# Filler products of TensorE and GpSimd's digit memsets moved in the routing stage of a mixture-of-experts layer

## The reference

```python
def moe_ffn(h, w_router, b_router, w1, b1, w2, b2):
    logits = jnp.matmul(h, w_router, preferred_element_type=jnp.float32) + b_router
    top_vals, top_idx = lax.top_k(logits, TOP_K)
    gates = jax.nn.softmax(top_vals, axis=-1)
    e_flat = top_idx.reshape(-1)
    order = jnp.argsort(e_flat, stable=True)
    ...
    def expert_block(args):
        toks, gts, e = args
        xb = h[toks]
        hid = xb @ w1[e] + b1[e]
        yb = clamped_swiglu(hid) @ w2[e] + b2[e]
        return yb * gts[:, None]
```

## Time and profile before

| | us |
|---|---|
| median of 3 runs | 1941.39 |
| lowest, highest | 1940.39, 1941.68 |
| profiled execution | 1941.4 |
| its span, first to last instruction | 1939.6 |
| TensorE busy in the span | 1895.6 |
| VectorE | 1357.6 |
| ScalarE | 415.9 |
| GpSimd | 238.5 |

### The profile page before, as it was taken

One profiled execution on the slowest core, in us unless ns is written; L12 is line 12 of the kernel. 1 busy time (PEld: TensorE's weight loads), 2 busy tenths in 40 slices (PEclk: granted clock), 3 DMA queues, 4 the chain that ended last, 5 costly groups with the idle time before them and its releaser, 6 DMA issues.

```text
span 1939.6 us, 33456 instructions
## 1 busy us (share of the span) xinstructions
PE 1895.6 (98%) x12202; PEld 1384.8 (71%) x12202; DVE 1357.6 (70%) x3838; ACT 415.9 (21%) x925; POOL 238.5 (12%) x319
## 2 busy tenths in 40 slices
PE   8999999997999999999999999999999999999996
PEld 6677777774999999999999999933334444444442
DVE  3777877874467777775666666665548788888785
ACT  2222333323022122222222222222322000001000
POOL 1222122221010011111111111110100000000000
PEclk9999999998999999999999999999999999999998
DMA  9411110014876787778888889889999999999891
GB/s 315 109 43 43 43 43 17 26 33 179 324 223 214 247 269 267 247 260 280 286 293 294 299 300 302 312 298 411 407 400 379 336 324 335 336 338 331 302 326 56
DMA packets 202864, 477.51 MB, mean 246 GB/s; under 512 B 7016, under 2 KB 14228, under 8 KB 196624
## 3 DMA queue, kind: packets, MB, share of 16 engines
q1 hardware_dynamic: 188048, 427.44, 61.2%
q0 software_dynamic: 11312, 39.85, 8.3%
q10 hardware_dynamic: 3452, 9.47, 1.2%
HBM read 449.33 MB, written 27.41 MB: 246 GB/s over the span
## 4 chain that ended last, share of the span: by engine, by line
issue 38%; PE 33%; DMA 4%; POOL 1%; DVE 0%; POOLq 0%; ACT 0%; DVEq 0%
PE ps_unit L1974 32%; DMA out_dram<-y_rows,idx_cur 4%; POOL x_got L1451 1%; PE ps_act L2086 0%; PE ps_list L2086 0%; PE ps_list L1946 0%; POOL carrier L1447 0%; POOL out_dram L1508 0%; POOLq L1144 0%; DVE match L1655 0%; POOLq L1344 0%; PE ps_unit L1954 0%; POOL out_dram L1463 0%; ACT xT L1559 0%; POOLq L1499 0%
## 5 line engine op out<-in xcount | busy, mean ns | idle before, releaser
L1974 PE MATMUL ps_unit<-xT,w_slot 128*128 128x136 f32 (+6 forms) x3840 | 521.5, 298 | 4.1 <-issue 2.6
L1974 PEld LDWEIGHTS ps_unit<-xT,w_slot 128*128 128x128 f32 x3840 | 516.7, 196 | 4.7 <-issue 4.7
L2004 PE MATMUL ps_unit<-w_slot,xT 128*128 128x512 f32 x704 | 306.7, 594 | 0.0
L1333 DVE STREAM_TRANSPOSE xT<-x_got 32x256 f32<-32x256 f32 x644 | 280.3, 435 | 10.6 <-DMA x_got<-h_rows,idx_next 2.2
L1974 PE MATMUL ps_unit<-act_T,w_slot 128*128 128x136 f32 (+6 forms) x1920 | 261.6, 298 | 0.1
L1974 PEld LDWEIGHTS ps_unit<-act_T,w_slot 128*128 128x128 f32 x1920 | 257.9, 190 | 2.2 <-DVE act_T L1736 1.5
L2004 PEld LDWEIGHTS ps_unit<-w_slot,xT 128*128 128x128 f32 x704 | 132.8, 190 | 163.0 <-issue 163.0
L1752 DVE STREAM_TRANSPOSE y_rows<-yT 32x256 f32<-32x256 f32 x372 | 162.0, 435 | 55.1 <-ACT yT L1574 50.2
L976 PE MATMUL ps_c<-hT,w_in_sb 128*128 128x128 f32 x1536 | 181.8, 278 | 3.5 <-DMA w_in_sb<-in_w_in_dram 3.5
L976 PEld LDWEIGHTS ps_c<-hT,w_in_sb 128*128 128x128 f32 x1536 | 176.9, 193 | 8.3 <-issue 4.0
L1447 POOL TENSOR_TENSOR carrier<-carrier 128x1 f32<-128x1 f32 x64 | 14.5, 227 | 1300.2 <-issue 613.6
(11 more groups left out here) (305 smaller groups left out, 1864.5 us busy)
## 6 DMA issues: line engine op xcount, KB each, us to landing
w_slot<-in_w_dram SPq DMA_DIRECT2D x192, 2048.0 KB, 12.3
w_in_sb<-in_w_in_dram SPq DMA_DIRECT2D x6, 1024.0 KB, 15.5
x_in<-in_x_dram SPq DMA_DIRECT2D x8, 512.0 KB, 3.6
x_res<-in_x_dram SPq DMA_DIRECT2D x8, 512.0 KB, 4.9
out_dram<-x ACTq DMA_DIRECT2D x8, 512.0 KB, 5.2
h_rows<-h ACTq DMA_DIRECT2D x8, 512.0 KB, 3.2
w_in_sb<-in_w_in_dram SPq DMA_DIRECT2D x2, 1536.0 KB, 10.2
w_out_sb<-in_w_out_dram SPq DMA_DIRECT2D x1, 2048.0 KB, 17.6
```

The source lines that it names most:

```text
L1333: last = nc.vector.transpose(out[c * Q:(c + 1) * Q, :, tokens], rows.rearrange("p (k c j) -> p k c j", c=P // Q, j=Q)[:, :, c, :])
L1974: last = pe.matmul(ps_unit[p % RING][:, u, 0:n], w, moving[:, k, 0:n], start=(k == 0), stop=(k == KD - 1))
L2004: last = pe.matmul(ps_hid[c], xT[:, k, 0:P], w_slot[:, c, k, :], start=(k == 0), stop=(k == KD - 1))
```

## The change

Five fillers behind the ranks become three. Two fillers are added between the bias transposes and the token lists, and two behind the last register load of a word, ahead of the loads of the job counts. On GpSimd the four memsets of the digits move from behind `recycled` to ahead of the clearing of the semaphores; the memset of `carrier` now carries `recycled` itself, and its own semaphore goes.

```diff
@@ gpsimd
             nc.gpsimd.tensor_tensor(gates_left[:], gates[:], gate_parts[:, :, 0, :], ALU.subtract).then_inc(parts_left, 1)
+            for i in range(DIGITS):
+                nc.gpsimd.memset(digits[:, i:i + 1], float(1 << BITS * i)).then_inc(digits_made, 1)
             pool.wait_ge(ranked, 1)
             pool.wait_ge(rstep.sem, 1)
             pool.sem_clear(mixer_sems)
...
-            pool.sem_inc(recycled, 1)
-            for i in range(DIGITS):
-                nc.gpsimd.memset(digits[:, i:i + 1], float(1 << BITS * i)).then_inc(digits_made, 1)
-            nc.gpsimd.memset(carrier[:], 0.0).then_inc(carrier_cleared, 1)
-            pool.wait_ge(carrier_cleared, 1)
+            nc.gpsimd.memset(carrier[:], 0.0).then_inc(recycled, 1)
+            pool.wait_ge(recycled, 1)
@@ tensor
-            hold_clock(5, ps_list[:])
+            hold_clock(3, ps_list[:])
...
             biases()
+            hold_clock(2)
             pe.wait_ge(table_ready, TABLES)
             list_tokens(0)
...
+            hold_clock(2)
             slim_jobs = pe.value_load(jobs[0:1, 2:3], min_val=0, max_val=most_jobs)
```

More of the change, by code:

```diff
@@ L1220, in experts @@
         biases_read = sem("biases_read")
-        carrier_cleared = sem("carrier_cleared")
         ends_taken = sem("ends_taken")
```

## The result

The changed kernel took 1946.47 us (median of 12 runs, 1942.14 to 1950.29) against 1941.96 us (12 runs, 1939.38 to 1945.34) for the one before: ratio 1.0021, 95% interval 1.0012 to 1.003. It is 4.5 us (0.2%) slower, where 1.5 us faster was forecast, and outside the range. Both kernels spread over some 6 to 8 us. The profiled execution of the changed kernel took 1942.8 us, near the low end of its runs, 1941.0 of it span, so its span is only 1.4 us longer than that of before. A good part of that nearness comes from the part of the program that did not change: the ranks start at 447.21 us in place of 450.26 (TensorE was busy for 45.1 of the first 50 us, against 42.0).

The account below looks back on a forecast made before the run. TensorE is busy 98% of the span; the routing chain to the first transposes, bounded by a code-fetching branch, was to shorten by 1.54 us, other edits costing nothing: 1941.4 - 1.54 = 1939.9 us, range 1938.3 to 1941.7.

Parts of the forecast that it names:

- The front: Routing stage behind the ranks: five fillers to three starts the order-key product at 455.03 instead of 456.57, gain 1.54 us.
- The digit memsets: GpSimd, moved ahead of the semaphore clear: 0.20 us there, costed at nothing; left in place they would cut the gain.
- The fillers ahead of the lists: Two fillers, four passes, between bias transposes and token lists: hidden at full clock, partly delaying the lists at half clock.
- Both ends: Fillers before the token lists: full clock, done 461.19, hidden; half clock, done 462.87, lists 0.55 us earlier instead of 1.54.
- it moves with the match: Branch before the first transposes: reached a fixed time behind the first match's wait, so it and the transposes come 1.54 us earlier.
- the long branch: Compare-and-branch skipping the largest size's job loop, ahead of the first transposes: 4637 ns, taken to be the bound, length unchanged.
- The branch as a fetch, not a wait for the fillers: Ahead of the first transposes: the 4.64 us branch fetches code, so queued fillers don't matter and the gain stays 1.54 us.
- The first rival: Branch ahead of the first transposes ends with the filler queue; with half-clock fillers gain 0.7 us, 1940.7 us; 17%.
- The place of the code: Loops behind two net added fillers lie elsewhere in memory: nothing in the forecast; as a rival, new size-switch gaps, 8%.
- The sum: Behind the first job TensorE runs back to back and moves as a block: 1941.4 - 1.54 = 1939.9 us.
- The third rival: Size switches of the wide matmul: two new gaps of 1.3 us from moved code, +1.1 us, 1942.5 us; 8%.
- three signs of being wrong: Branch length changing over half a microsecond, order-key product later than 455.3, or new gaps besides the switches at 607.6 and 833.4.

Follow-up runs that it names:

- the front alone: Three fillers behind the ranks, early digit memsets, `recycled` on the carrier's memset, two fillers in a never-run loop, against the kernel before: 1939.08 us, -2.57.
- the best kernel: Changed kernel without the fillers ahead of the lists, plus 16 never-run fillers, against the kernel before: 1935.92 us (-6.50), repeated 1938.12 us (-3.07).
- place +2: Kernel before with two never-run fillers that move the later loops by two fillers, against the kernel before: 1943.5 us, +1.85.
- place +16: Changed kernel with 14 never-run fillers, so later loops lie 16 fillers further on, against the kernel before: 1937.86 us, -4.05.

## Why the prediction was wrong

**The front: right.** The order-key product was put 455.03 - 450.26 = 4.77 us behind the ranks; in eleven of the fourteen profiles with three fillers it stands at 4.92 to 4.98, in the others at 5.35 to 5.71, where the clock came back late (the changed kernel's own profile is one: 5.67, all six passes at 0.85 us). Before, it stood at 6.31, 6.30 and 7.42. The gain of 1.54 us was the size for one state of the clock, and in the changed kernel's own profile only 0.64 of it came; without the fillers ahead of them the lists stand 11.9 us behind the ranks in all but one profile, against 13.2 to 14.3 before. The digit memsets were ready in time, as costed: in the changed kernel the digit product starts 0.32 us behind the order-key product, and the carrier's memset ends at 453.38, ahead of the bias transposes at 454.73.

**The fillers ahead of the lists: the wrong end of the step, and a wrong link behind it.** Both ends were worked out (hidden at full clock; at half clock the lists 0.55 us ahead of today's), and the case said to be harmless. Half clock came, for the whole of the pair or much of it, in five of seven profiles. The lists begin 0.2 to 1.6 us behind the match with this pair, 1.0 in the mean of seven, and 0.15 in every profile without it: 0.85 us of delay. In the changed kernel's profile the clock had fallen before the pair began and the lists came 0.8 us later than before the change. The step that failed was "it moves with the match": I took the register loads and the long branch to run ahead of the fillers. They don't run ahead of the lists. The branch is taken up 4.1 to 4.3 us behind the start of the lists in every kernel:

```profile
L2117 PEldq TENSOR_LOAD <-ends x3: 301/314/484, 461.3 to 463.1; - x3
...
L2051 PEldq COMPARE_BRANCH  x2: 84/2636/5187, 465.5 to 471.0; - x2
```

The first load starts at 461.3, 0.1 us behind the lists at 461.20, although the match was there at 459.6. So late lists make a late branch and late transposes: 24.2 us where 21.2 had been forecast, of which 2.4 us are the late lists (13.99 against 461.88 - 450.26 = 11.62; 0.9 of it because the match itself came late, 1.5 by the pair) and 0.6 us a longer branch (5187 ns against 4637; it is 4.4 to 5.9 us in all profiles, with no pattern that I can name).

**The branch as a fetch, not a wait for the fillers: supported.** The time from the last filler to the end of the branch should have been fixed if the branch waited for them. It was 1.0 us before and 1.2 us in the changed kernel, but 2.1 us in the front alone, and in the first run of the best kernel the branch (taken up at 463.0, 4520 ns) had ended at 467.5, a microsecond ahead of the last filler's end at 468.57. The first rival, the branch ending with the queue of fillers, is out with that. What the last case also shows is that the fillers can be the later of the two; the prediction had them done ahead of it in both cases.

**The place of the code: put at nothing in the forecast, and given 8% as a rival.** The sum said that behind the first job all of TensorE's work moves as a block; it took 3.0 us more instead. The third rival named the size switches, took 1.3 us a gap, wanted two new ones, and came to 1942.5 us. No new gap appeared. The two there were grew by 0.34 and 0.93 us, and behind the longer one TensorE's clock fell, which cost 1.76 us more on the next 96 passes. Missing from the price was that second effect. The argument against it, that the program moves by little, was no argument: eight instructions moved the time by 1.9 us (by 3.4 in the profile), 64 by 3.4 us the other way. That 1942.5 lies nearer to the measured time than the forecast does is in part luck: no new gap came, and its sum has no loss by the pair. Of the three signs of being wrong that the prediction named, two came: a branch 0.55 us longer, and the order-key product 5.67 us behind the ranks, where 455.3 was 5.04; the third, new gaps, did not.

**The sum, as it came out.** By medians: front -2.6, place +2 of +1.9, last pair near 0, together -0.7, against -1.3 measured for the kernel that has just these three. The whole change averages +2.1 over four measurements, so the pair ahead of the lists would cost 3.4 us by this comparison, made across chips and from +0.4 to +5.8 by single measurements. At the place +16 it comes to 0.7 us (-4.05 against the mean, -4.8, of the best kernel's two). The profiles show 0.85 us of delay of the lists by it in the mean, and transposes at 22.9 us behind the ranks with the pair against 22.2 without. That the pair costs something is shown by these lists; how much, and what else made the first measurement 4.5 us, stays open: with and without the pair were never measured on one chip at one place.

## What to carry to other kernels

When a change adds or removes instructions ahead of loops that are entered by branches, test it beside dead code of the same length, and try a few lengths: here dead code alone was worth from +1.9 to -3.4 us, more than the 1.5 us that the change was forecast to bring. Fillers belong where the engine would wait anyway for longer than they take at half clock; ahead of the very product that others wait for, what they take beyond the wait is paid when the clock happens to be down. For effects of a thousandth, compare stretches of the profile that the change can reach beside the medians, and in several executions: the one profile of the front alone shows no gain where its median is 2.6 us lower.

## What the runs showed of the hardware that was not expected

- A compare-and-branch of TensorE's sequencer at a size switch lasts 0.24 us or 2.5 to 3.0 us by where the code lies (243 ns before, 2812 ns with two dead fillers, 2905 ns in the changed kernel). A short one doesn't mean that nothing stalls: before, 2.35 us passed behind it without a record. The Trainium skill, page "Runtime: NRT & Kernel Launch", section "Instruction fetch mechanics", says that a taken branch out of the loaded code forces a fetch of the target before execution goes on; the long branches agree with that, the size of the block that it gives was not tested here beyond the one displacement of 256 instructions.
- A pause of TensorE of 2.1 to 2.6 us, with full clock ahead of it, was followed by half clock in all eight profiles that have it at the second switch; pauses of 1.3 to 1.6 us there were not, in any of four, nor those of up to 2.0 us at the first switch.
- The sequencer passes the match's semaphore (459.6 us) but takes up the next register load only when the products behind it begin (461.3 us, changed kernel).
- The same kernel differs by up to 5 us between four measurements against the same reference kernel; two of their four profiles show one more fall of the clock at 1298 us, behind a longer wait for gathered rows, 3.3 us of the rest.
